# Ends of stages rearranged in a two-layer diffusion block: half-slice waits, bank pairs, matrices loaded in the down stage, three vectors turned as rows

## What is computed

```python
for i in range(2):                       # layer 0: attention, layer 1: Fourier mixing
    sh1, sc1, g1, sh2, sc2, g2 = split(silu(c) @ ada_w[i] + ada_b[i], 6)
    h = rms_norm(x, norm_mix_g[i]) * (1 + sc1) + sh1          # x: 256 x 2048
    if i == 0:
        o = attention(h, h_ctx) @ w_o                         # 16 heads, 4 kv heads, 256 context tokens
    else:
        o = fftn(h.reshape(256, 8, 256), axes=(0, 2), norm="ortho").real.reshape(256, 2048) @ fourier_w_o
    x = x + g1 * o
    m = rms_norm(x, norm_mlp_g[i]) * (1 + sc2) + sh2
    x = x + g2 * (square(relu(m @ w1[i])) @ w2[i])            # w1: 2048 x 8192, w2: 8192 x 2048
return rms_norm(x, final_norm_g)
```

## Time and profile before

| what | value |
|---|---|
| time, median of 3 executions | 2156.29 us (2152.25 to 2159.48) |
| the profiled execution: time | 2154.51 us |
| its span, first to last instruction | 2152.7 us |
| TensorE busy | 2033.4 us, 94% of the span |
| VectorE, ScalarE busy | 64%, 45% |
| mean granted TensorE clock | 0.974 of full |
| moved by DMA | 539 MB, 250 GB/s over the span |

### The profile page before, as it was taken

One profiled execution on the slowest core, in us unless ns is written; L12 is line 12 of the kernel. 1 busy time (PEld: TensorE's weight loads), 2 busy tenths in 40 slices (PEclk: granted clock), 3 DMA queues, 4 the chain that ended last, 5 costly groups with the idle time before them and its releaser, 6 DMA issues.

```text
span 2152.7 us, 25259 instructions
## 1 busy us (share of the span) xinstructions
PE 2033.4 (94%) x10396; PEld 1664.5 (77%) x10396; DVE 1378.5 (64%) x1379; ACT 977.0 (45%) x1284; POOL 109.1 (5%) x196
## 2 busy tenths in 40 slices
PE   4999879898999999999999979999999999999997
PEld 2677656666888878788888868778888887888885
DVE  2466779836867867577657766875665544555555
ACT  4433555424544454444444444354554554444443
POOL 1111000110000000000000000000000000000000
PEclk8999989999999999999999989999999999999999
DMA  9798427786988979588668825957777555555652
GB/s 369 277 339 321 171 91 248 287 339 212 348 293 298 358 276 349 206 320 326 248 215 325 329 86 217 380 184 238 251 237 251 181 172 176 195 195 195 215 191 102
DMA packets 140682, 538.89 MB, mean 250 GB/s; under 512 B 8436, under 2 KB 9620, under 8 KB 101012
## 3 DMA queue, kind: packets, MB, share of 16 engines
q1 hardware_dynamic: 106576, 329.73, 43.5%
q0 software_dynamic: 31744, 201.34, 25.5%
q10 hardware_dynamic: 2248, 6.21, 0.8%
HBM read 535.15 MB, written 2.10 MB: 250 GB/s over the span
## 4 chain that ended last, share of the span: by engine, by line
PE 84%; DVE 8%; ACT 2%; DMA 2%; issue 2%; POOL 0%; DVEq 0%; SPq 0%; ACTq 0%; POOLq 0%
PE ps L1459 22%; PE ps L1415 12%; PE ps L1419 12%; PE ps L1418 12%; PE ps L1461 11%; PE ps L1279 4%; PE ps L1280 4%; PE ps L1281 4%; DVE sum_wo L840 1%; PE ps L1320 1%; DVE ada_sum L840 1%; DMA c_rows<-in_ctx 1%; DVE x_tm L1096 1%; DVE gated L1094 1%; DVE w_lo L815 1%
## 5 line engine op out<-in xcount | busy, mean ns | idle before, releaser
L815 DVE TENSOR_TENSOR w_lo<-raw,w_hi 128x1024 fp32r<-128x1024 f32 x624 | 760.2, 1223 | 599.2 <-ACT w_hi L451 599.2
L451 ACT ACTIVATE w_hi<-raw 128x1024 fp32r<-128x1024 f32 x624 | 657.9, 1058 | 915.7 <-PE ps L1419 426.1
L1459 PE MATMUL ps<-hh,w_hi 128*128 128x512 f32 x2048 | 726.8, 399 | 2.5 <-ACT g_row L604 1.4
L1461 PE MATMUL ps<-hh,w_lo 128*128 128x256 f32 x2048 | 576.5, 282 | 0.0
L1415 PE MATMUL ps<-w_hi,hh 128*128 128x512 f32 x1152 | 451.3, 392 | 13.3 <-DVE w_lo L815 7.6
L1459 PEld LDWEIGHTS ps<-hh,w_hi 128*128 128x128 f32 x2048 | 386.5, 189 | 98.6 <-ACT g_row L604 3.0
L1419 PE MATMUL ps<-w_hi,hh 128*128 128x512 f32 x1152 | 450.7, 391 | 0.0
L1418 PE MATMUL ps<-w_lo,hh 128*128 128x512 f32 x1152 | 450.7, 391 | 0.0
L1461 PEld LDWEIGHTS ps<-hh,w_lo 128*128 128x128 f32 x2048 | 388.9, 190 | 0.0
L1415 PEld LDWEIGHTS ps<-w_hi,hh 128*128 128x128 f32 x1152 | 217.8, 189 | 61.2 <-issue 13.0
L1419 PEld LDWEIGHTS ps<-w_hi,hh 128*128 128x128 f32 x1152 | 217.6, 189 | 45.7
(11 more groups left out here) (184 smaller groups left out, 1383.2 us busy)
## 6 DMA issues: line engine op xcount, KB each, us to landing
raw<-in_mlp_w SPq DMA_DIRECT2D x256, 1024.0 KB, 5.3
ada_raw<-in_ada_w POOLq DMA_DIRECT2D x161, 1024.0 KB, 5.3
raw<-in_attn_w_qkv SPq DMA_DIRECT2D x24, 1024.0 KB, 10.3
spare<-in_ada_w POOLq DMA_DIRECT2D x22, 1024.0 KB, 9.6
raw<-in_attn_w_o SPq DMA_DIRECT2D x16, 1024.0 KB, 5.8
raw<-in_fourier_w_o SPq DMA_DIRECT2D x16, 1024.0 KB, 4.9
g_row<-in_ada_w POOLq DMA_DIRECT2D x9, 1024.0 KB, 10.6
x_tm<-in_x ACTq DMA_DIRECT2D x2, 1024.0 KB, 7.7
```

Source lines behind the costliest of these rows:

```text
L451: act.activation(w_hi[:, s % SPLIT, :], raw[:, piece % RAW, s % 2, :], ACT.Copy).then_inc(hi_ready, 1)
L815: nc.vector.tensor_tensor(w_lo[:, s % SPLIT, :], raw[:, s // 2 % RAW, s % 2, :], w_hi[:, s % SPLIT, :].bitcast(F32), ALU.subtract).then_in ...
L1459: mm(ps[:, bank, :].rearrange("p (a t) -> p a t", a=2), w_hi[:, s % SPLIT, w], hh[:, k, :, :], start=(k == 0), stop=False, skip_group_chec ...
L1461: ins = mm(ps[:, bank, 0:T], w_lo[:, s % SPLIT, w], h_hi[:, k, :], start=False, stop=(k == KT - 1), skip_group_check=True)
```

## The change

The edits have these parts:
- `rows_last` waits for the third of its four slices before banks 0 and 1 of a half, and for the fourth only before banks 2 and 3.
- At stage ends VectorE gates and ScalarE squares banks in pairs (0+1, 2+3, 4+5, then 6 and 7 singly), and the order in `stage_end` is new: the split of the next stage's first slice no longer stands in the middle of VectorE's list but at its end, and the total of the second half comes between two normalised blocks. At the last stage end half of the output is scaled before the second total.
- In the output projection the pair of banks 0 and 1 is gated at VectorE's k = 2 (before: bank 0 at k = 1, bank 1 at k = 2), and TensorE's scale pieces wait for both.
- The DFT matrices are loaded at slice 88 of layer 0's down stage and split at slice 104. Vector 7's steps are spread over 41 slices, not 45.
- The first four slices of the Fourier projection are split in steps 2 to 5 of the Fourier loop.
- Vectors 1, 3 and 5 are turned by `lay_rows` (four matmuls with 512 moving columns on strips of 32), a copy by ScalarE, and, two or three slices later, `pick_cols` (four matmuls with 4 columns). TensorE waits for VectorE's addition at the end of blocks 5 and 15.

```diff
+LAID = {1: 4, 3: 6, 5: 7}
...
+def picks(l):
+
+    return {45: 3, 125: 5} if l == 0 else {}
...
-    gated = place("gated", [P, 2, 512], F32, shared)
-    junk = place("junk", [P, 2, 512], F32, shared + 4096)
+    gated = place("gated", [P, 2, 1024], F32, shared)
+    junk = place("junk", [P, 1024], F32, shared + 45056)
...
+    PAIRS = ((0, 2), (2, 2), (4, 2), (6, 1), (7, 1))
...
+        def square_banks(q, j, n):
...
+            act.wait_ge(x_blk, 8 * q + j + n)
+            if op or q:
...
+            act.activation(junk[:, at:at + 512 * n], x_tm[:, tt, 512 * nb:512 * (nb + n)], ACT.Square,
+                           accum_out=ss[:, 4 * tt + part:4 * tt + part + 1]).then_inc(sq_done, 1)
 
...
 
             if q:
-                for j in range(4):
-                    square_bank(q, j)
+                square_banks(q, 0, 2)
+                square_banks(q, 2, 2)
                 root_of(q, 0)
-            square_bank(q, 4)
-            square_bank(q, 5)
+            square_banks(q, 4, 2)
             if q == 0:
                 root_of(q, 0)
             if next_first:
                 split_hi(next_first)
-            square_bank(q, 6)
-            square_bank(q, 7)
+            square_banks(q, 6, 1)
+            square_banks(q, 7, 1)
             root_of(q, 1)
...
-                act.wait_ge(ulo_ready, 32)
-                act.dma_start(dft[:, :, :], dft_in.rearrange("(k p) n -> p k n", p=P)).then_inc(dft_in_sem, 16)
-                split_hi(2 * P_WO[1] + 1)
-                act.wait_ge(dft_in_sem, 16)
-                act.activation(dft_hi[:, :, :], dft[:, :, :], ACT.Copy).then_inc(dft_hi_ready, 1)
...
+                    if 2 <= g < 6:
+                        split_hi(2 * P_WO[1] + g - 2)
                 row_out(6, range(2, 4), 4)
-                split_hi(2 * P_WO[1] + 2)
-                split_hi(2 * P_WO[1] + 3)
...
-                    if 2 <= k < 6:
-                        square_bank(0, k - 2)
+                    if k in (3, 5):
+                        square_banks(0, k - 3, 2)
+                    if k == 7:
+                        act.wait_ge(rows_T, 1)
+                        act.activation(ada_rows[:, :], ps[:, 1, :], ACT.Copy).then_inc(rows_copied, 1)
...
+                act.wait_ge(col_T, 1)
                 act.activation(ada_rows[:, :], ps[:, 0, :], ACT.Copy).then_inc(rows_copied, 1)
...
+                if s in turns(l) and turns(l)[s] in LAID:
+                    v = turns(l)[s]
+                    act.wait_ge(rows_T, LAID[v] - 4)
+                    act.activation(ada_rows[:, :], ps[:, 4 * ((blk + 1) % 2), :], ACT.Copy).then_inc(rows_copied, 1)
...
+                if l == 0 and s == 88:
+                    act.wait_ge(ulo_ready, 18)
+                    act.dma_start(dft[:, :, :], dft_in.rearrange("(k p) n -> p k n", p=P)).then_inc(dft_in_sem, 16)
+                if l == 0 and s == 104:
+                    act.wait_ge(dft_in_sem, 16)
+                    act.activation(dft_hi[:, :, :], dft[:, :, :], ACT.Copy).then_inc(dft_hi_ready, 1)
...
-            stage_end(2 * l + 1, 2 * P_WO[1] if l == 0 else None)
+            stage_end(2 * l + 1, None)
...
+            if v in LAID:
+                nc.vector.tensor_tensor(mod_col[:, col:col + 16].rearrange("p (j f) -> p j f", j=4),
+                                        ps[:, bank, 0:16].rearrange("p (f j) -> p j f", j=4),
+                                        bias_col[:, col:col + 16].rearrange("p (j f) -> p j f", j=4), ALU.add).then_inc(mod_ready, 1)
...
-        def gate_bank(q, j):
+        def gate_banks(q, j, n):
 
...
+            cols = slice(512 * nb, 512 * (nb + n))
+            last, op = j + n - 1, PAIRS.index((j, n))
...
+            elif last < 7:
+                dve.wait_ge(bank_full, 7 * q - 1 + last + 1)
...
-            nc.vector.tensor_tensor(gated[:, j % 2, :], ps[:, bank, :], g_row[:, cols], ALU.mult).then_inc(gated_ready, 1)
-            dve.wait_ge(gated_ready, 8 * q + j + 1)
-            nc.vector.tensor_tensor(x_tm[:, tt, cols], x_tm[:, tt, cols], gated[:, j % 2, :], ALU.add).then_inc(x_blk, 1)
+            buf = gated[:, op % 2, 0:512 * n]
+            nc.vector.tensor_tensor(buf.rearrange("p (a t) -> p a t", a=n), ps[:, bank:bank + n, :],
+                                    g_row[:, cols].rearrange("p (a t) -> p a t", a=n), ALU.mult).then_inc(gated_ready, 1)
+            dve.wait_ge(gated_ready, 5 * q + op + 1)
+            nc.vector.tensor_tensor(x_tm[:, tt, cols], x_tm[:, tt, cols], buf, ALU.add).then_inc(x_blk, n)
...
-            dve.wait_ge(sq_done, 8 * q + (4 * tt + 4 if q else (6, 8)[tt]))
-            nc.vector.tensor_reduce(rstd[:, tt, 0:1], ss[:, 4 * tt:4 * tt + 4], AX_X, ALU.add).then_inc(ss_ready, 1)
+            dve.wait_ge(sq_done, 5 * q + (5 if tt else 2 if q else 3))
+            nc.vector.tensor_reduce(rstd[:, tt, 0:1], ss[:, 4 * tt:4 * tt + 2 + tt], AX_X, ALU.add).then_inc(ss_ready, 1)
...
         def stage_end(q, next_first, middle=None):
 
-            for j in range(0 if q else 4, 5):
-                gate_bank(q, j)
             if q:
-                total(q, 0)
-            gate_bank(q, 5)
-            if q == 0:
-                total(q, 0)
-            if next_first:
-                split_lo(next_first)
-            invert(q, 0)
-            gate_bank(q, 6)
-            gate_bank(q, 7)
+                gate_banks(q, 0, 2)
+                gate_banks(q, 2, 2)
+            gate_banks(q, 4, 2)
+            total(q, 0)
+            gate_banks(q, 6, 1)
+            gate_banks(q, 7, 1)
             if middle:
                 middle()
-            for b in range(4):
-                if q < 3:
-                    normed(q, 0, b)
-            total(q, 1)
-            invert(q, 1)
-            for b in range(4):
-                if q < 3:
+            invert(q, 0)
+            if q == 3:
+                scaled(0, 0)
+                scaled(0, 1)
+                total(q, 1)
+                scaled(0, 2)
+                scaled(0, 3)
+                invert(q, 1)
+                for b in range(4):
+                    scaled(1, b)
+            else:
+                normed(q, 0, 0)
+                normed(q, 0, 1)
+                total(q, 1)
+                normed(q, 0, 2)
+                normed(q, 0, 3)
+                invert(q, 1)
+                for b in range(4):
                     normed(q, 1, b)
+                if next_first:
+                    split_lo(next_first)
...
-                split_lo(2 * P_WO[1] + 1)
-                dve.wait_ge(dft_hi_ready, 1)
-                nc.vector.tensor_tensor(dft_lo[:, :, :], dft[:, :, :], dft_hi[:, :, :].bitcast(F32),
-                                        ALU.subtract).then_inc(dft_ready, 1)
                 h_split(1, 0)
                 h_split(1, 1)
...
-                split_lo(2 * P_WO[1] + 2)
-                split_lo(2 * P_WO[1] + 3)
+                    if 2 <= g < 6:
+                        split_lo(2 * P_WO[1] + g - 2)
...
-                    if 1 <= k < 5:
-                        gate_bank(0, k - 1)
-                    if k == 8:
+                    if k in (2, 4):
+                        gate_banks(0, k - 2, 2)
+                    if k == 9:
                         take_col(1, 1)
...
+                if s in picks(l):
+                    take_col(picks(l)[s], 4 * ((blk + 1) % 2))
...
+                if l == 0 and s == 104:
+                    dve.wait_ge(dft_hi_ready, 1)
+                    nc.vector.tensor_tensor(dft_lo[:, :, :], dft[:, :, :], dft_hi[:, :, :].bitcast(F32),
+                                            ALU.subtract).then_inc(dft_ready, 1)
...
-                if l == 0 and s >= 78 and (s - 78) * 16 // 45 > (s - 79) * 16 // 45 and (s - 78) * 16 // 45 < KT:
-                    ada_step(7, (s - 78) * 16 // 45)
-            stage_end(2 * l + 1, 2 * P_WO[1] if l == 0 else None, (lambda: take_col(7, 7)) if l == 0 else None)
-
-        dve.wait_ge(fin_in, 16)
-        for tt in range(2):
-            for b in range(4):
-                cols = slice(512 * b, 512 * (b + 1))
-                nc.vector.scalar_tensor_tensor(y_rows[:, tt, cols], x_tm[:, tt, cols], rstd[:, tt, 1:2], late_row[:, cols],
-                                               ALU.mult, ALU.mult).then_inc(fin_out, 1)
+                if l == 0 and s >= 78 and (s - 78) * 16 // 41 > (s - 79) * 16 // 41 and (s - 78) * 16 // 41 < KT:
+                    ada_step(7, (s - 78) * 16 // 41)
+            if l == 1:
+                dve.wait_ge(fin_in, 16)
+            stage_end(2 * l + 1, None, (lambda: take_col(7, 7)) if l == 0 else None)
...
+        def lay_rows(v, bank):
+
+            pe.wait_ge(ada_used, summed_before(KT * v) + KT)
+            for j in range(4):
+                ins = mm(ps[32 * j:32 * j + 32, bank, :], ones[:, 0:32], sum_of(v)[:, 512 * j:512 * (j + 1)], start=True, stop=True,
+                         skip_group_check=True)
+            ins.then_inc(rows_T, 1)
+
+        def pick_cols(v, bank):
+
```

(23 more changed lines are left out.)

39 lines of the change are left out of this document (20 added, 19 removed).

## The result

The changed kernel takes 2134.01 us, the median of 6 runs (2128.54 to 2139.68); the kernel before took 2156.32 beside it (6 runs). The ratio over all these runs is 0.9904, interval 0.9887 to 0.9920, which is 20.7 us less (17 to 24); the two medians by themselves are 22.3 apart. The forecast was 2129, the range 2119 to 2140.

The account below looks back on a forecast made before the run. TensorE, busy 94% of the span, was taken as the bound, with losses at turns, waits and joints. Terms -13.2 + 5.4 - 1.0 - 10.7 - 2.7 - 4.6 = -26.8 gave 2129 us as median; range 2119 to 2140.

Parts of the forecast that it names:

- the new wait: Output projection: TensorE idle 4 to 5 us before the first scale piece, released by VectorE's addition to x.
- the third end: Fourier projection to up: three gate pairs and a moved split save 2.7 us; VectorE's modulation-sum steps stay untouched.
- Vector 1: Turning this modulation vector by laid rows instead of one-column matmuls saves 3.2 us, slow clock included.
- Vectors 3 and 5: Turning these modulation vectors by laid rows saves 4.9 and 5.1 us, slow clock behind the old turns included.
- Bank pair: Output projection: gating banks 0 and 1 together delays TensorE's scale pieces, costing 5.4 us (bounds 3.75 and 6.2).
- First end: Output projection to up: VectorE's new order starts the second half's normalisation sooner; 1.0 us saved.
- Second end: Down to Fourier: earlier last matrices, paired banks and DFT matrices moved into the down stage save 10.7 us.
- half-slice waits: Last matrices: TensorE goes on without stopping for the last slice; a rival said no gain, 2138 us, chance 0.10.
- the third rival: No new wait at the scale pieces, or Fourier matmuls start at full clock: -33 us, 2123 us, chance 0.12.
- Fourth end: Output stage end: TensorE 4.4 us earlier, half the rows normalised before the last total; 4.6 us saved.
- the clock falls behind laid rows or stays low longer: Rival: slow clock behind laid vectors or the output projection's new idle; some -21 us, 2135 us, chance 0.12.
- the transfers: Rival: from slice 78 of the down stage the queues cannot bring the data; +43 us, 2172 us, chance 0.03.

Follow-up runs that it names:

- e3: Changed kernel with vectors 1, 3 and 5 turned as one-column matmuls again; ratio 0.9935 to the kernel before.
- e1: Changed kernel with bank 0 gated alone in the output projection and TensorE's first scale piece waiting for it only; ratio 0.9867 to the kernel before, 2128.1 us.
- the second profile: The changed kernel run and profiled again, unaltered; ratio 0.9910 to the kernel before, span 2134.5 us.
- e4: Changed kernel with the DFT matrices fetched and split at the second stage end, as before the change; ratio 0.9907 to the kernel before.
- e2: Changed kernel with TensorE waiting for the whole last slice's low half before the last two matrices at three stage ends; ratio 0.9911 to the kernel before.
- e5: Changed kernel with banks 0 and 1 gated ahead of the last step of vector 8's sum at the third stage end; ratio 0.9896 to the kernel before.
- e6: Changed kernel with each down stage started on the token half whose banks are already free; ratio 0.9855 to the kernel before.

## Why the prediction was right

The sign, the new wait and the place of each gain but one (the third end) were as forecast; the sum was 26.8 and the ratio gives 20.7, so 6 us of the forecast did not come. Term by term, from the table:

- **Vector 1**: 3.2 forecast, 3.6 by e3.
- **Vectors 3 and 5**: 10.0 forecast. The up stage is 7.4 shorter, but its first 4.6 us now run at half clock, which takes 2.3: 9.7. The clock that I had booked as saved behind vector 5 fell, however, one joint later, at the start of the down stage, for 1.6. At that joint TensorE idled 2.4 us before and idles 2.6 now. This is the first step that failed: I took a fall of the clock as the turn's own and asked only whether laid rows would cause one.
- **Bank pair** (and its place behind the low half of slice 6): 5.4 forecast, 6.5 by e1. The idle was 3.85 longer as forecast (3.75); the clock was low for longer than behind any wait in the rows, 2.6 instead of 1.7. In the second profile it was 1.2 less.
- **First end**: 1.0 forecast. Scale to up gives 71.5 - 3.6 - 66.7 = 1.2 (by e1). But the clock is still low when the up stage begins, as said, so 1.1 is lost instead. Windows of the stage's first 4.6 us, after and before:

```profile
514.92:519.50 4.58, 4.58 (x14) 0.50 0.76 242
```

```profile
514.51:519.10 4.59, 4.59 (x28) 1.00 0.77 238
```

- **Second end**: 10.7 forecast. Down to F was 407.6 and is 399.0, 397.4 without the clock at the down stage's start: 10.2. By single profiles e4 puts 4.9 of it on the DFT and e2 2.7 on the half-slice waits; the other 2.6 are left for the pairs and the new order, which no run tests alone. The size was near, the inside was not. I had the first Fourier matmul 20.2 us behind the start of the last matrices, and it came after 22.05, as the clock fell during the turn of vector 7 and the row turn behind it took 3.76 us (1.96 before). In return the Fourier loop started at full clock, which was half of the third rival. In e1 it is the other way round, 20.1 and a slow start of the loop, and the whole stretch from last to F is the same within 0.1 (59.9 and 60.0). The changed kernel's rows:

```profile
1243.67 4.16 PE L1440 MATMUL ps<-ones,sum_down 128*128 128x1 f32 x32
1247.69 3.76 PE L1463 MATMUL ps<-ada_sum,ones 128*128 128x512 f32 x4
...
1254.70 0.36 PE L1319 MATMUL ps<-dft_hi,hh 128*128 128x260 f32 x1 [1.54 <-DVE hh L1149]
```

- **Third end**: 2.7 forecast, none found. F to the second down stage, less the step, is 472.3 before, 472.9 and 473.1 in the two profiles after. I wrote that the change doesn't touch the two steps of the sum that VectorE does ahead of its gates. But the second of them now waited 2.70 for its weights and not 1.17, so that the gates began 89.0 us after F instead of 87.4; then TensorE waited 3.1 for the second pair and, at half clock, turned vector 8 in 6.98 us, 4.54 before. This is the second step that failed. e5 shows that the late gates cost 1.6 to 3.2 us of this end; it doesn't separate the wait for the weights from the clock behind it.
- **Fourth end**: 4.6 forecast. Down to end is 5.6 shorter, 1.6 of it a fall of the clock at the start of the down stage of before, which the second profile after has too: 4.0, and e2's profile puts all of it on the half-slice waits (4.2), so nothing is left for the scalings ahead of the second total.

So the joints together: -3.6 - 9.7 + 1.6 + 6.5 - 1.2 + 2.3 - 10.2 + 0.6 - 4.0 = -17.7. In the profiled pair three things beside the change add to it: the start, 1.2 (3.85 of its 445.6 being the new wait), the step, 5.1, and the clock in the second down stage, 1.6: -25.6, against 26.0 in the spans. These three differ between two profiles of the same kernel. The ratios, 20.7 and (0.9910) 19.4, have 17.7 inside both their intervals (17 to 24 and 15 to 23), as they should if the three fall out anew in each run; that they do so over many runs is not shown. The profiled pair, 26.0, is near my 26.8 by luck.

Of the rivals, the first, "the clock falls behind laid rows or stays low longer", gave 2135, which is nearer to the 2134.0 measured than my 2129, and it came true in part. Behind the new idle the clock cost 2.6 us and not 1.7, and behind vector 5's laid rows it fell in two profiles of seven, where the rival had looked for it, behind 2 us of idle. The rest of what was missing it didn't name: the slow starts of stages (1.6 and 2.3) and the third end (2.7). The half-slice waits did gain by the trace (e2), the transfers cost nothing (without a fall of the clock at its start the down stage takes 337.4, as in e1, and before the change it took 340.1 with a wait of 2.56 in it), and the new wait came (e1). The chances as listed add up to 0.93 for faster and 0.04 for no change, not to the 0.94 and 0.03 that I gave.

The Trainium skill ("TensorE: Matmul & The Clock Gate", "What's actually happening") says that the clock gate is set by how busy the array has recently been. I had read this as saying that a back-to-back turn would cost no clock, and the trace disagrees with that reading: in e3 the turn of vector 1, busy for all of its 3.61 us, is followed by 3.4 us at 0.51.

## What to carry to other kernels

Price the clock by joint, with all its waits, and not by the edit: here some of the slow clock that an edit removed came back at the next place where TensorE idled. Joining two gates and additions into one saved VectorE some 0.2 us of 2.7 for two banks, but the first result came 1.1 us later, and 2.7 more because the pair has to stand where its second bank is ready; so look for who waits for the first. When a busy engine waits for a buffer to drain, as at the down stages, let it start on what is free: that alone was worth over half of what the change brought (e6). Take a gain of a few us from the trace, but say so when the total time doesn't show it, as with e2 and e4 here.

## What was not expected of the hardware

- The matmul pair of 512 and 256 columns has two steady steps, 347 and 353 ns, at a granted clock of 1.00, each kept for hundreds of pairs. It is switched at a joint, partly by chance: up to 9.6 us here, with identical code 4.4 and 7.8. The three matmuls of 512 columns of the down stages stayed at 680 ns in all profiles.
- How long the clock stays low behind a wait is not told by the wait: 6.8 and 3.4 us behind the same 4.9 us in two profiles of the same kernel, 1.2 us apart in cost. Where a joint became shorter, as at the first end here, part of the slow stretch was found in the next stage.
